# Attention values with the values stationary in every stage, two heads alternating, and the last stage's result turned back

## The reference, cut to what matters

```python
outs_a.append(jnp.einsum('bhqk,bkhd->bqhd', p_a.astype(v_a.dtype), v_a[:, :kend]))   # layer 0, 8 heads
outs_b.append(jnp.einsum('bhqk,bkhd->bqhd', w_b.astype(v_b.dtype), v_b[:, :kend]))   # layer 0, 8 heads
...
parts = [jnp.einsum('bnhqk,bnkhd->bnqhd', p[..., i * CHUNK:(i + 1) * CHUNK], v_p[:, i:i + n_chunks])
         for i in range(LEFT_CHUNKS + 1)]                                            # layer 1, 16 heads
...
branches = jnp.stack([o_a.reshape(b, s, W_BR) * jax.nn.silu(ga),                     # third block: 8 heads of
                      o_b.reshape(b, s, W_BR) * jax.nn.silu(gb),                     # branch a, 3 x 8 of branch b,
                      o_c.reshape(b, s, W_BR) * jax.nn.silu(gc)], axis=2)            # 8 of branch c: five groups
```

## Time and profile before

| | |
|---|---|
| median of 3 runs | 1051.57 us (1049.77 to 1051.69) |
| the profiled execution: its time | 1051.47 us |
| the profiled execution: its span | 1049.5 us |
| PE busy | 998.5 us, 95% of the span |
| DVE busy | 633.9 us, 60% |
| ACT busy | 593.0 us, 57% |
| the chain that ended last | 89% of it on PE, 5% ACT, 4% DVE |
| mean granted TensorE clock | 0.995 |

### The profile page before, as it was taken

One profiled execution on the slowest core, in us unless ns is written; L12 is line 12 of the kernel. 1 busy time (PEld: TensorE's weight loads), 2 busy tenths in 40 slices (PEclk: granted clock), 3 DMA queues, 4 the chain that ended last, 5 costly groups with the idle time before them and its releaser, 6 DMA issues.

```text
span 1049.5 us, 13511 instructions
## 1 busy us (share of the span) xinstructions
PE 998.5 (95%) x5026; PEld 816.8 (78%) x5026; DVE 633.9 (60%) x780; ACT 593.0 (57%) x912; POOL 21.3 (2%) x21
## 2 busy tenths in 40 slices
PE   4999789999998999989999998999999998999998
PEld 3888668888887777768888887788787886778876
DVE  3576567555555574665555555668567566766654
ACT  4677464544454564554544454666756575856561
POOL 1000004000000000010000000000000000000000
PEclk9999999999999999999999999999999999999999
DMA  7435156655655433368555655454343333335550
GB/s 232 146 117 200 41 200 193 207 188 173 200 162 198 161 123 121 118 212 291 197 190 171 200 163 197 145 177 161 126 154 120 120 121 121 121 121 200 176 185 40
DMA packets 105691, 170.23 MB, mean 162 GB/s; under 512 B 3843, under 2 KB 65210, under 8 KB 105652
## 3 DMA queue, kind: packets, MB, share of 16 engines
q1 hardware_dynamic: 103040, 161.23, 46.6%
q0 software_dynamic: 2288, 8.37, 2.3%
q10 hardware_dynamic: 324, 0.10, 0.0%
HBM read 168.58 MB, written 1.11 MB: 162 GB/s over the span
## 4 chain that ended last, share of the span: by engine, by line
PE 89%; ACT 5%; DVE 4%; issue 1%; DMA 0%; ACTq 0%; DVEq 0%
PE acc L442 14%; PE acc L402 13%; PE acc L404 12%; PE acc L403 12%; PE pair_ps L404 7%; PE pair_ps L402 7%; PE pair_ps L403 7%; PE acc L612 4%; PE turn_ps L524 2%; PE pair_ps L512 1%; PE acc L492 1%; PE pair_ps L511 1%; ACT w_hi L922 1%; PE turn_ps L460 1%; ACT logit L1045 1%
## 5 line engine op out<-in xcount | busy, mean ns | idle before, releaser
L1538 DVE TENSOR_TENSOR w_lo<-w_raw,w_hi 128x2048 fp32r<-128x2048 f32 (+3 forms) x156 | 351.2, 2256 | 154.6 <-ACT w_hi L922 154.2
L922 ACT ACTIVATE w_hi<-w_raw 128x2048 fp32r<-128x2048 f32 (+3 forms) x156 | 290.3, 1863 | 86.8 <-PE acc L404 47.4
L402 PE MATMUL acc<-w_hi,uT_hi 128*128 128x512 f32 (+3 forms) x552 | 221.3, 401 | 9.9 <-DVE w_lo L1538 6.0
L404 PE MATMUL acc<-w_hi,uT_lo 128*128 128x512 f32 (+3 forms) x552 | 213.8, 387 | 0.0
L403 PE MATMUL acc<-w_lo,uT_hi 128*128 128x512 f32 (+3 forms) x552 | 213.2, 386 | 0.0
L402 PEld LDWEIGHTS acc<-w_hi,uT_hi 128*128 128x128 f32 x552 | 105.2, 191 | 35.1 <-issue 8.9
L402 PE MATMUL pair_ps<-w_hi,uT_hi 128*128 128x512 f32 x320 | 126.6, 396 | 0.0
L404 PE MATMUL pair_ps<-w_hi,uT_lo 128*128 128x512 f32 x320 | 125.0, 391 | 0.0
L403 PE MATMUL pair_ps<-w_lo,uT_hi 128*128 128x512 f32 x320 | 124.7, 390 | 0.0
L404 PEld LDWEIGHTS acc<-w_hi,uT_lo 128*128 128x128 f32 x552 | 104.8, 190 | 21.4
L403 PEld LDWEIGHTS acc<-w_lo,uT_hi 128*128 128x128 f32 x552 | 105.3, 191 | 18.1
(11 more groups left out here) (210 smaller groups left out, 1269.0 us busy)
## 6 DMA issues: line engine op xcount, KB each, us to landing
w_raw<-in_w_in SPq DMA_DIRECT2D x46, 1024.0 KB
w_raw<-in_w_gate SPq DMA_DIRECT2D x44, 512.0 KB
w_raw<-in_w_up SPq DMA_DIRECT2D x44, 512.0 KB
w_raw<-in_w_down SPq DMA_DIRECT2D x22, 1024.0 KB
w_raw<-in_w_out SPq DMA_DIRECT2D x12, 1024.0 KB
w_raw<-in_w_qkv SPq DMA_DIRECT2D x16, 512.0 KB
w_raw<-in_w_branch SPq DMA_DIRECT2D x6, 1024.0 KB
w_raw<-in_w_in SPq DMA_DIRECT2D x10, 512.0 KB
```

The costliest lines, as they stand in the source:

```text
L402: mm(o, xh, wh[:, k, :], start=first and k == 0, stop=False)
L404: done = mm(o, xl, wh[:, k, :], start=False, stop=last and k == len(kts) - 1)
L922: activation(w_hi[:, slot, 0:width], w_raw[:, slot, 0:width], ACT.Copy).then_inc(hi_done, 1)
L1538: v.tensor_tensor(w_lo[:, slot, 0:width], w_raw[:, slot, 0:width], w_hi[:, slot, 0:width].bitcast(f32), ALU.subtract).then_inc(lo_done, 1)
```

## The change

Both forms become one. In every stage the values are the stationary operand (128x64). For a pair and token block 0 of the keys, each head has one matmul over all 256 columns of queries; for block 1, one over the last 128 columns. The order is head 0, head 1, head 0, head 1; head j writes partitions 64j to 64j+63 of `out_ps`.

In the third block the result now has channels on the partitions and has to be turned. ACT copies it to SBUF (`copy_outputs`, into spare columns of `heads` or `bias`), PE transposes it back with two 128x128 transposes into columns 256 to 511 of the same bank (`turn_outputs`), and DVE copies that to `heads` as before, from the other columns. PE turns pair `s-3` in the middle of unit `s`, and pair 3 after unit 5. ACT copies pair `s-3` as the first thing of step `s`, before `slot_step`, and pair 3 at the end of step 5. DVE's `token_outputs` move from pair `s-2` to pair `s-3` at the end of step `s`, behind `maxima(s)` and `copy_probs(s-1)`; pair 3 is read at the end of step 5. `values(t)` waits for `out_read` of pair `t-1` as before.

```diff
@@ PE, values
-                for j in range(2):
-                    c0 = P * (t % 4) + HD * j
-                    v0, v1 = [(v_mla[:, blk, c0:c0 + HD] if kind == "mla" else qkv[:, 2, blk, c0:c0 + HD])
-                              for blk in range(TB)]
-                    pr = prT[:, t % 2, j, :]
-                    if kind != "last":
-
-                        o = out_ps[HD * j:HD * j + HD, 0:S]
-                        mm(o[:, 0:128], v0, pr[:, 0:128], start=True, stop=True)
-                        mm(o[:, 128:256], v0, pr[:, 128:256], start=True, stop=False)
-                        done = mm(o[:, 128:256], v1, pr[:, 256:384], start=False, stop=True)
-                        continue
-                    o0, o1 = out_ps[:, HD * j:HD * j + HD], out_ps[:, P + HD * j:P + HD * j + HD]
-                    mm(o0, pr[:, 0:128], v0, start=True, stop=True)
-                    mm(o1, pr[:, 128:256], v0, start=True, stop=False)
-                    done = mm(o1, pr[:, 256:384], v1, start=False, stop=True)
+                for blk in range(TB):
+                    for j in range(2):
+                        c0 = P * (t % 4) + HD * j
+                        v = v_mla[:, blk, c0:c0 + HD] if kind == "mla" else qkv[:, 2, blk, c0:c0 + HD]
+                        done = mm(out_ps[HD * j:HD * j + HD, P * blk:S], v,
+                                  prT[:, t % 2, j, S * blk:S * blk + S - P * blk],
+                                  start=blk == 0, stop=blk == 1, skip_group_check=True)
                 done.then_inc(out_done, 1)
+
+            def turn_outputs(t, pair0, outs):
+
+                pe.wait_ge(out_copied, pair0 + (t + 1) - 16)
+                for blk in range(TB):
+                    done = transpose(out_ps[:, S + P * blk:S + P * blk + P], outs[t % 2][:, P * blk:P * blk + P], ident[:, :])
+                done.then_inc(out_turned, 1)
@@ PE, project_and_attend
+                            if s >= 3 and blk == 1:
+                                turn_outputs(s - 3, pair0, outs)
                             if s == 5 and blk == 1:
                                 attention_step(kind, 5, pair0, turn0)
...
+                turn_outputs(3, pair0, outs)
@@ ACT, project_and_attend
+                def copy_outputs(t):
+
+                    act.wait_ge(out_done, pair0 + (t + 1))
+                    activation(outs[t % 2], out_ps[:, 0:S], ACT.Copy).then_inc(out_copied, 1)
...
                 for s in range(6):
+                    if 3 <= s:
+                        copy_outputs(s - 3)
                     if s < 2 * len(chunks):
                         slot_step(prefetch[s])
...
+                    if s == 5:
+                        copy_outputs(3)
@@ DVE, token_outputs
-                dve.wait_ge(out_done, pair0 + (t + 1))
-                o = out_ps[:, 0:S].rearrange("p (b n d) -> p b n d", b=TB, n=2)
+                dve.wait_ge(out_turned, pair0 + (t + 1) - 16)
+                o = out_ps[:, S:2 * S].rearrange("p (b n d) -> p b n d", b=TB, n=2)
@@ DVE, attention_step
-                if kind == "last" and 2 <= s:
-                    token_outputs(s - 2, pair0, head0)
@@ DVE, project_and_attend
                     attention_step(kind, s, n.pair, head0, bias_of)
+                    if 3 <= s:
+                        token_outputs(s - 3, n.pair, head0)
+                    if s == 5:
+                        token_outputs(3, n.pair, head0)
```

More of the change, by code:

```diff
@@ L147, in build_program @@
         m_strict = flat_heads[:, 4608:4864]
+        head_outs = [heads[:, i, 32:36, :].rearrange("p n d -> p (n d)") for i in range(2)]
+        window_outs = [flat_bias[:, 5120 + S * i:5120 + S * i + S] for i in range(2)]
         ones = flat_heads[:, 4864:5120]
@@ L207, in build_program @@
         out_read = sem("out_read")
+        out_copied = sem("out_copied")
+        out_turned = sem("out_turned")
         proj_done = sem("proj_done")
@@ L564, in project, with project_and_attend @@
                     chunk(uT_hi, uT_lo, KT, width)
-            def project_and_attend(widths, kind, qk, copied):
+            def project_and_attend(widths, kind, qk, copied, outs=head_outs):
                 pair0, turn0 = n.pair, n.turn
@@ L854, in _ @@
             project_and_attend((512, 512, 256), "last", 9, 54)
-            project_and_attend((512, 512, 512), "last", 11, 60)
+            project_and_attend((512, 512, 512), "last", 11, 60, window_outs)
             def merged_tile(kt0):
@@ L1056, in round_outputs, with attention_step @@
                 activation(oT_hi[:, kt0 + t, :], out_ps[:, 0:S], ACT.Copy).then_inc(out_hi, 1)
-            def attention_step(kind, s, pair0, head0, kt0=None):
-                if kt0 is not None and 3 <= s:
-                    round_outputs(s - 3, pair0, kt0)
+            def attention_step(kind, s, pair0, head0):
                 if 1 <= s < 5:
@@ L1077, in project, with project_and_attend @@
                     later = done()
-            def project_and_attend(chunks, kind, head0=0, gains=None, prefetch=(UNIT,) * 6, after={}, kt0=None):
+            def project_and_attend(chunks, kind, head0=0, gains=None, prefetch=(UNIT,) * 6, after={}, outs=head_outs):
                 pair0 = n.pair
+                def copy_outputs(t):
+                    act.wait_ge(out_done, pair0 + (t + 1))
+                    activation(outs[t % 2], out_ps[:, 0:S], ACT.Copy).then_inc(out_copied, 1)
                 if kind == "last":
@@ L1091, in project_and_attend @@
                         copy_pair(kind, t, pair0)
-                    attention_step(kind, s, pair0, head0, kt0)
+                    attention_step(kind, s, pair0, head0)
                     if s == 1:
@@ L1495, in _ @@
                                prefetch=(UNIT, UNIT, 1024, 1024, UNIT, UNIT))
-            project_and_attend([swish_gate(1), swish_gate(2), lambda: gate_exponentials(0)], "last", 32, 8,
+            project_and_attend([swish_gate(1), swish_gate(2), lambda: gate_exponentials(0)], "last", 32, 8, outs=window_outs,
                                after={3: factors(0, 1, 4), 5: lambda: split_banks(oT_hi, 0, 4, turn_banks)})
```

## The result

| | kernel before | changed kernel |
|---|---|---|
| median | 1050.67 us (4 runs, 1049.62 to 1051.69) | 1084.16 us (4 runs, 1083.15 to 1084.61) |
| ratio, 95% interval | | 1.0297 [1.0269, 1.0325] |
| span of the profiled execution | 1049.5 us | 1082.7 us |
| mean granted TensorE clock | 0.995 | 0.981 |

The changed kernel is slower: 3.0% by the ratio, 33.5 us between the two medians. The prediction was 1074.0 with a range of 1068 to 1080: the sign was right, the size was 10 us short and outside the range.

What follows compares the result with a forecast made beforehand. PE was taken to bound the kernel (busy 95%, 89% of the chain). Third block 5 x 5.26 + 0.7 = 27.0 us, less 4.5 from the early layers, is 22.5; on 1051.5 that makes 1074.0, range 1068 to 1080.

Steps and rivals of the forecast that it cites:

- The products: Values products on PE: 0.80 us a pair, against 1.08 in layers 0 and 1 and 1.26 in the third block.
- alternating: Order of heads in PE's products: lets both start at once, 0.80 us a pair; 1.08 if it helps nothing.
- The turning: PE's transposes in the third block: 0.11 us each, 0.22 for two, 4.4 us for 20 pairs.
- The rival with 0.27 us for each transpose: PE's turning: each transpose takes 0.27 us, not 0.11; 6.4 us more, 1080; 5% shared with alternating bringing no overlap.
- The new waits: PE ahead of values at steps 3, 4, 5 waits for DVE's output read: about 2.3, 1.2, 2.1 us.
- +5.26 a group: Third block: each group of the loop ends 5.26 us later, with waits, product gains and turning counted.
- The early layers: Layers 0 and 1: 16 pairs gain 0.28 us each from the new products, 4.5 us together.
- The clock falls: Rival, third block: half clock behind each group's first or last wait, 3 to 7 us more, 1077 to 1081; 10%.
- Faster: Rival, third block: DVE's read does not hold up PE, only products and turning count, 1043; 2%.

Runs made afterwards that it cites:

- the early layers alone: The kernel before, with the new form of the products only in layers 0 and 1, third block unchanged: 1050.46 us, 0.9978.
- the waits filled: The changed kernel, with 10, 5 and 8 idle PE products ahead of the products of pairs 1, 2 and 3 in third-block groups: 1074.01 us, 1.0205.
- The two kernels with the read moved: The changed kernel with DVE's output read ahead of maxima and probabilities, 1062.44 us; additionally ahead of the head norm and, at step 5, slot_step, 1051.70 us.
- DVE's read first: The changed kernel, with DVE's read of pair s-3 ahead of the maxima and probabilities of step s: 1062.44 us, 1.0087.
- the two orders: The kernel before with new products in layers 0 and 1 only: heads alternating, 1050.46 us; one head after the other, 1048.78 us.
- step 3 filled: The changed kernel, with ten idle PE products only ahead of the product of pair 1 in third-block groups: 1078.03 us, 1.023.

## Why the prediction was right in its sign and wrong in its size

**The products, right.** 0.80 us for each pair, in both stages. The support for it (alternating) was not needed.

**The turning, right.** 0.22 us for two. The rival with 0.27 us for each transpose is out.

**The new waits, right.** The idle times forecast for steps 3, 4 and 5 were about 2.3, 1.2 and 2.1 us; in group 3 they are 2.38, 1.14 and 1.85. At step 5 one link of the chain was priced a little too high: from the end of the product (837.92 + 0.87) to the start of ACT's rounding (839.11) 0.32 us pass, where the sum has 0.42. (The half unit of group 4 is shorter by 12 times 0.11, 1.3 us and not 1.4; it changes nothing.) Predicted was +5.26 a group, and 5.16 is measured with the waits filled; predicted 27.0 for the third block, measured 26.1 there.

**The early layers, right in kind, twice too high.** Predicted 4.5. The starts of DVE's `w_lo` copies tell where the time is gained. The 109th, at the start of the third block, comes 3.1 us earlier than before with the early layers alone, 3.5 in the changed kernel, 3.9 with the waits filled. But the 11th, at 72 us and so ahead of the first product of probabilities and values at 81, already comes 0.9, 1.2 and 1.4 us earlier, which the change can't have done. From the 11th to the 109th 2.2, 2.3 and 2.5 us are gained, and 2.0 to 2.5 in seven of the eight profiles of other kernels than the one before. (In the eighth, the changed kernel once more, 3.5 us are lost: there PE waits 4.05 us for DVE at 167 with a stretch behind it.) Of these some 1.5 to 1.9 come in layer 0, where 2.2 were predicted, and only about 0.5 in layer 1, where it was 2.2 as well. Around 418 to 421 the changed kernel has a stretch that the kernel before does not have. The kernel before has one at 656 instead, but there it costs nothing that shows: from the 101st copy to the 109th 51.1 us pass in both. The stretch at 418 would cost about what is missing, but no run here separates it.

**The step that failed: "The clock falls".** The sum held no term for the clock; it was a rival at 10%, sized "3 to 7 us in all, 1077 to 1081". It should have been in the sum. It came, with seven stretches in the first trace and six in the second, behind the ten waits of steps 3 and 5 and never behind the five of step 4, and it cost 10.2 us by the filled kernel (1084.16 - 1074.01; against the changed kernel measured beside it, 1083.67, it is 9.7). The price of one stretch, 1.5 us, was right; the number of stretches was too low, since it was taken as "each group's first or last" wait. What was set against it was no evidence: that DVE was idle for 2.1 us says nothing of PE, and a single idle time of PE of 1.63 us without an effect says little of fifteen with up to 3.2. The one row that spoke to the point was the earlier trace rows, and it spoke for it. With the low clock kept away, the changed kernel takes 1074.01 us, the predicted time. That it is met so closely is in part luck: the early layers gave some 2 us less than the sum has, the third block cost 0.9 less, and the kernel before beside this run took 1053.49 us and not 1051.5.

The Trainium skill, in "TensorE: Matmul & The Clock Gate", Part 1, has the clock cut to half or given in full by how busy PE has been of late. The table above agrees: with the same waits, idle in one kernel and filled in the other, it is 8 stretches against 1.

**The range** reached to 1080 because the clock case was cut at its edge and given one chance in ten. **Faster** was rightly small: the read stands behind `maxima` in DVE's list, and that decided it. The two kernels with the read moved show that almost all of the loss hung on this: 1084.16, 1062.44, 1051.70.

## What to carry to other kernels

Where a change lets the engine that bounds the kernel wait for another, follow the instruction that releases it through the list of its own engine: DVE had 2.3 us to spare right ahead of it and still held PE up, and moving three reads of 0.42 us a group was worth 32 us. Where PE is to stand still again and again, put the low clock behind the waits into the sum, with the number of waits times the price of one stretch as the upper end (1.3 to 1.6 us each; here six or seven of ten waits of 2.1 us or more in the changed kernel, but one of five with DVE's read first), and not beside it as a rival. The part of the change that may be worth keeping is the smaller one, the four instructions for each head in the early layers: some 2 us in the profiles, 0.9978 [0.9957, 0.9999] and 0.9965 [0.9944, 0.9985] in the times of the two orders.

## What was not expected of the hardware

- The same kernel drops its clock behind other waits in another execution: 721.8 and 790.0 in groups 1 and 2 of the first trace, behind step 3 and step 5; in the second trace it was step 5 (from 741.9) and step 3 (779.5). The number is nearly the same, 8 and 7 in the third block, and so is the median time, 1084.16 and 1083.67.
- The length of a wait alone does not say whether the clock falls behind it. The wait of step 5, 2.1 us long in groups 1 to 3, had a stretch behind it in two of three groups in the first trace of the changed kernel, in two of three with step 3 filled, and in none with DVE's read first. The transposes of step 4 in group 4 wait 2.02 us for ACT in both kernels with the read moved, and only the first of them has a stretch there.
- The clock does not fall at a fixed place behind a wait: the product that ends the wait at 827.91 already runs slow (1.48 us); after the wait that ends at 843.82 the product takes its 0.80, and the work behind it is slow from 844.62 on.
- Idle products cost nothing that shows here and gave 10 us back; the time is still 2.05% [1.85, 2.24] above the kernel before.
